# Turning h before the first mixer: a trip through DRAM and 32x32 turns on VectorE, in place of TensorE's transposes, with the norm vector in the split of w_in

## The reference, cut to what matters

```python
h = swiglu_half_step(h, ffn1_norm[i], ffn1_w_gate_up[i], ffn1_w_down[i])
z = rms_norm(h, mix_norm[i]) @ w_in[i]
z_mix, z_mem = z[..., :768], z[..., 768:]
y_mix = multiscale_pool_mixer(z_mix, pool_w[i], pool_scale[i])       # layer 0
y_mem = memory_attention(z_mem, mem, mem_norm[i], w_mem_kv[i], ...)
h = h + concatenate([y_mix, y_mem]) @ w_out[i]
```

## Time and profile before

| | us |
|---|---|
| median of 3 runs | 912.81 |
| lowest, highest run | 912.79, 912.90 |
| the profiled execution: its time | 912.87 |
| the profiled execution: its span | 910.8 |
| TensorE busy | 905.8 |
| VectorE busy | 635.5 |
| ScalarE busy | 501.3 |
| GpSimd busy | 107.2 |

### The profile page before, as it was taken

The page is one execution under the profiler, slowest core; times in us unless marked ns, Lnnn a source line. Parts: engine busy times, 40 slices in busy tenths (PEclk is TensorE's granted clock), DMA queues, the critical chain, the costliest instruction groups (busy, mean ns, idle before and its releaser), DMA issues.

```text
span 910.8 us, 15058 instructions
## 1 busy us (share of the span) xinstructions
PE 905.8 (99%) x4998; PEld 769.0 (84%) x4998; DVE 635.5 (70%) x970; ACT 501.3 (55%) x750; POOL 107.2 (12%) x186
## 2 busy tenths in 40 slices
PE   9999999999999999999999999999999999999998
PEld 6888888888888888888888888888888788888887
DVE  6766577687677766566778766656878776666665
ACT  6654455565655554454564645445676664545542
POOL 2052302003000000000002930000121000000000
PEclk9999999999999999999999999999999999999999
DMA  9897656556346656565375865665443276566551
GB/s 294 268 278 231 196 187 183 186 157 212 88 141 201 213 173 201 184 194 195 119 213 164 265 199 173 208 185 185 141 137 117 76 243 214 183 206 188 171 171 47
DMA packets 140195, 168.26 MB, mean 185 GB/s; under 512 B 12488, under 2 KB 104624, under 8 KB 140160
## 3 DMA queue, kind: packets, MB, share of 16 engines
q1 hardware_dynamic: 135616, 164.67, 56.9%
q0 software_dynamic: 4368, 3.07, 1.6%
q10 hardware_dynamic: 176, 0.07, 0.0%
HBM read 166.19 MB, written 1.05 MB: 184 GB/s over the span
## 4 chain that ended last, share of the span: by engine, by line
PE 99%; DVE 1%; ACT 0%; issue 0%; POOL 0%; ACTq 0%; POOLq 0%
PE ps L1763 35%; PE ps L1768 18%; PE ps L1977 8%; PE ps L1975 8%; PE ps L1973 8%; PE ps L1849 5%; PE ps L1851 5%; PE ps L1850 5%; PE ps L1733 1%; PE ps L2101 1%; PE ps L1802 1%; PE ps L2182 1%; PE ps L2070 0%; PE ps L1816 0%; PE ps L2139 0%; PE ps L2236 0%
## 5 line engine op out<-in xcount | busy, mean ns | idle before, releaser
L1763 PE MATMUL ps<-mainT,w_hi 128*128 128x512 f32 x1376 | 468.7, 393 | 0.2
L1148 DVE TENSOR_TENSOR w_lo<-w_raw,w_hi 128x1024 fp32r<-128x1024 f32 x296 | 350.7, 1221 | 42.6 <-ACT w_hi L739 42.2
L1768 PE MATMUL ps<-mainT,w_lo 128*128 128x256 f32 x1376 | 350.5, 280 | 0.0
L739 ACT CAST w_hi<-w_raw 128x1024 fp32r<-128x1024 f32 x296 | 299.7, 1047 | 28.3 <-PE ps L1763 11.2
L1763 PEld LDWEIGHTS ps<-mainT,w_hi 128*128 128x128 f32 x1376 | 248.9, 188 | 46.2 <-issue 0.5
L1768 PEld LDWEIGHTS ps<-mainT,w_lo 128*128 128x128 f32 x1376 | 255.8, 189 | 13.8
L797 ACT COPY gate_up_f<-ps 128x512 f32<-128x512 f32 x88 | 51.2, 582 | 105.0 <-PE ps L1763 99.6
L1240 DVE TENSOR_TENSOR gate_up_f<-ps,gate_up_f 128x256 f32<-128x256 f32 x88 | 37.2, 423 | 90.5 <-ACT gate_up_f L797 90.4
L1977 PE MATMUL ps<-w_hi,actT_lo 128*128 128x512 f32 x320 | 98.9, 390 | 0.0
L1975 PE MATMUL ps<-w_lo,actT_hi 128*128 128x512 f32 x320 | 98.9, 390 | 0.0
L1973 PE MATMUL ps<-w_hi,actT_hi 128*128 128x512 f32 x320 | 98.6, 389 | 0.0
(11 more groups left out here) (248 smaller groups left out, 844.0 us busy)
## 6 DMA issues: line engine op xcount, KB each, us to landing
w_raw<-in_ffn_w_gate_up_dram SPq DMA_DIRECT2D x352, 256.0 KB, 3.9
w_raw<-in_ffn_w_down_dram SPq DMA_DIRECT2D x176, 256.0 KB, 3.5
w_raw<-in_w_in_dram SPq DMA_DIRECT2D x32, 256.0 KB, 3.5
w_raw<-in_w_out_dram SPq DMA_DIRECT2D x32, 256.0 KB, 3.4
w_raw<-in_w_mem_kv_dram SPq DMA_DIRECT2D x16, 256.0 KB, 3.0
w_raw<-in_w_kv_dram SPq DMA_DIRECT2D x8, 256.0 KB, 3.5
ycat<-in_mem_dram SPq DMA_DIRECT2D x1, 1024.0 KB, 7.5
z<-in_mem_dram POOLq DMA_DIRECT2D x32, 32.0 KB, 4.1
```

What stands on the lines that cost most here:

```text
L739: ins = nc.scalar.copy(half(w_hi[s], b), half(w_raw[s], b))
L1148: ins = nc.vector.tensor_tensor(half(w_lo[s], b), half(w_raw[s], b), half(w_hi[s], b).bitcast(F32), ALU.subtract)
L1763: return pe.matmul(gate_sums(fb, j)[:, :, tokens], w_hi[units[k // 4][0]][:, k % 4, cols], both[:, k, :, tokens], start=start, stop=stop)
L1768: return pe.matmul(gate_sums(fb, j)[:, 0, tokens], w_lo[units[k // 4][0]][:, k % 4, cols], both[:, k, 0, tokens], start=False, stop=False)
```

## The change

For the norm H2 alone, TensorE's 16 transposes of h and VectorE's four multiplications by the norm vector go. In their place GpSimd, for one token tile after the other, waits for both halves of h, writes the tile (512 KB) to a tensor `h_rows` in DRAM, waits until this has landed, and issues four DMAs of 128 KB that read it back in blocks of 32 tokens by 32 columns into z, one DMA for each group of 32 partitions. The reads are made of 1024 runs of 128 bytes each. This stands ahead of `row_roots("H2")` on GpSimd. VectorE turns the blocks from z into ycat, two instructions of 128x512 a tile (`h_turns`), and ScalarE and VectorE split from there. The norm vector goes into the split of w_in's four units. On VectorE and ScalarE the work around it is put in another order, as the diff shows: on VectorE the turns and splits of tile 0 stand between the low parts of z0b's first and second unit, and the turns of tile 1 between the two halves of the second unit.

```diff
--- before.py
+++ after.py
@@ -113,14 +113,14 @@
 GAINS = 9
 FIRST_GAINS = 2
 
-WEIGHT_GAIN = {"mkv0": 2, "mkv1": 3}
-
-SPLIT_GAIN = {"H0": 0, "H45": 1, "H2": 4, "H7": 5, "H3": 6, "H8": 7, "K45": 8}
+WEIGHT_GAIN = {"mkv0": 2, "mkv1": 3, "z0a": 4, "z0b": 4}
+
+SPLIT_GAIN = {"H0": 0, "H45": 1, "H7": 5, "H3": 6, "H8": 7, "K45": 8}
 
 
 SUMS = ["H0", "M", "H2", "H3", "H45", "H7", "H8"]
-TURNS = ["H0", "H2", "H3", "H45", "H7", "Y1", "H8"]
-SCALES = ["H0", "H2", "H3", "K45", "H45", "H7", "H8"]
+TURNS = ["H0", "H3", "H45", "H7", "Y1", "H8"]
+SCALES = ["H0", "H3", "K45", "H45", "H7", "H8"]
 SPLITS = ["H0", "M", "H2", "H3", "K45", "H45", "H7", "Y1", "H8"]
 SPLIT_INTO = {"M": "side", "Y1": "y", "K45": "y"}
 
@@ -212,6 +212,9 @@
         h = sb("h", [P, NT, D])
         z = sb("z", [P, NT, D])
         ycat = sb("ycat", [P, NT, D])
+        h_blocks = [z[:, t, :].rearrange("p (k i c) -> p k i c", i=P // BLOCK, c=BLOCK) for t in range(NT)]
+        h_turned = [ycat[:, t, :].rearrange("p (k t) -> p k t", t=P) for t in range(NT)]
+        h_rows = nc.dram_tensor("h_rows", [S, D], F32, kind="Internal").ap()
         mem_blocks = z[:, :, :].rearrange("p t d -> p (t d)").rearrange("p (k t) -> p k t", t=S)
         key_blocks = ycat[:, 0, 0:NT * KVH * HD].rearrange("p (t c) -> p t c", t=NT)
         key_rows = ycat[:, 1, :].rearrange("p (n t) -> p n t", n=KVH)
@@ -284,6 +287,9 @@
         mem_blocks_landed = sem("mem_blocks_landed")
         mem_blocks_turned = sem("mem_blocks_turned")
         keys_landed = sem("keys_landed")
+        h_rows_landed = sem("h_rows_landed")
+        h_blocks_landed = sem("h_blocks_landed")
+        h_blocks_turned = [sem(f"h_blocks_turned{t}") for t in range(NT)]
         consts_landed = sem("consts_landed")
         ident_landed = sem("ident_landed")
         gains_landed = [sem(f"gains_landed{g}") for g in range(2)]
@@ -451,6 +457,8 @@
         def turned_view(name, t, b):
             if name == "M":
                 return mem_turned[b][:, :, t * P:(t + 1) * P]
+            if name == "H2":
+                return h_turned[t][:, 4 * b:4 * b + 4, :]
             return ps[:, turn_bank(name, t, b), :].rearrange("p (k t) -> p k t", k=4)
 
         def slots(r):
@@ -697,6 +705,16 @@
                             pool.dma_start(mem_blocks[q * BLOCK:(q + 1) * BLOCK, k, :].rearrange("f (i c) -> f i c", c=BLOCK),
                                            mem_tokens[:, :, cols]).then_inc(mem_blocks_landed, 16)
             row_roots("M")
+            for t in range(NT):
+                rows = slice(t * P, (t + 1) * P)
+                for b in range(2):
+                    pool.wait_ge(h_ready[t][b], STEP_OF["H2"])
+                pool.dma_start(h_rows[rows, :], h[:, t, :]).then_inc(h_rows_landed, 16)
+                pool.wait_ge(h_rows_landed, 16 * (t + 1))
+                tokens = h_rows[rows, :].rearrange("(i f) (k q c) -> q f k i c", f=BLOCK, q=BLOCKS, c=BLOCK)
+                for q in range(BLOCKS):
+                    pool.dma_start(h_blocks[t][q * BLOCK:(q + 1) * BLOCK, :, :, :],
+                                   tokens[q]).then_inc(h_blocks_landed, 16)
             row_roots("H2")
             head_roots("mk0")
             pool.wait_ge(consts_landed, 16 * SMALL_LOADS)
@@ -777,6 +795,9 @@
                 elif name == "M":
                     act.wait_ge(mem_blocks_turned, b + 1)
                     src = turned_view(name, t, b)
+                elif name == "H2":
+                    act.wait_ge(h_blocks_turned[t], b + 1)
+                    src = turned_view(name, t, b)
                 else:
                     act.wait_ge(turned[t][b], turn_no(name))
                     src = turned_view(name, t, b)
@@ -901,6 +922,11 @@
                                act_f[:, :, :].rearrange("p c n -> p (c n)")).then_inc(actT_hi_ready, 1)
                 if FOLLOWING[name] is not None:
                     high_unit(FOLLOWING[name], 1)
+                    if after == "H2":
+                        row_sum(after, 0)
+                        high_unit("z0b", 0)
+                        row_sum(after, 1)
+                        return
                     into = "K45" if after == "H45" else after
                     split(into, 0, 0)
                     row_sum(after, 0)
@@ -1045,8 +1071,11 @@
                 split(after, 1, 1)
 
             ffn(0, "H0", "H2")
-            high_unit("z0b", 0)
+            split("H2", 0, 0)
+            split("H2", 0, 1)
             high_unit("z0b", 1)
+            split("H2", 1, 0)
+            split("H2", 1, 1)
             high_unit("z0a", 0)
             z_copy(0, 1, 0)
             high_unit("z0a", 1)
@@ -1356,6 +1385,11 @@
                 low_unit(FOLLOWING[name], 1, (0,))
                 residual(r, norm, 0, 0)
                 residual(r, norm, 0, 1)
+                if after == "H2":
+                    low_unit(FOLLOWING[name], 1, (1,))
+                    residual(r, norm, 1, 0)
+                    residual(r, norm, 1, 1)
+                    return
                 scale(into, 0, 0)
                 split(into, 0, 0)
                 low_unit(FOLLOWING[name], 1, (1,))
@@ -1618,10 +1652,24 @@
                                                scalar=row_scale("H2", t), in1=zp_hi[:, t, cols].bitcast(F32),
                                                op0=ALU.mult, op1=ALU.subtract).then_inc(pool_lo_ready, 1)
 
+            def h_turns(t):
+
+                dve.wait_ge(h_blocks_landed, 16 * BLOCKS * (t + 1))
+                for b in range(2):
+                    nc.vector.transpose(ycat[:, t, b * 512:(b + 1) * 512], z[:, t, b * 512:(b + 1) * 512]).then_inc(
+                        h_blocks_turned[t], 1)
+
             low_unit("z0b", 0)
             mkv0 = (mkv_sb, mkv_done, mkv_ready, 0, "mkv0", "M", GU_BANK)
+            h_turns(0)
+            split("H2", 0, 0)
+            split("H2", 0, 1)
+            low_unit("z0b", 1, (0,))
             kv_copy(*mkv0, 0)
-            low_unit("z0b", 1)
+            h_turns(1)
+            low_unit("z0b", 1, (1,))
+            split("H2", 1, 0)
+            split("H2", 1, 1)
             kv_copy(*mkv0, 1)
             dve.wait_ge(mkv_ready, NT)
             head_sums("mk0")
@@ -2027,9 +2075,11 @@
                     end_bank(1, 0)
                     last_halves()
                     return
-                turn_h(after, 0, 0)
+                if after != "H2":
+                    turn_h(after, 0, 0)
                 end_bank(1, 0)
-                turn_h(after, 0, 1)
+                if after != "H2":
+                    turn_h(after, 0, 1)
                 end_bank(1, 1)
 
             def turn_heads(y):
@@ -2244,7 +2294,7 @@
             turn_first(1, 0)
             keep_warm(WARM_PRODUCTS[1])
             ffn(0, "H0", "H2")
-            projection("mkv0", "side", "M", GU_BANK, mkv_done, 0, late_tile("H2"))
+            projection("mkv0", "side", "M", GU_BANK, mkv_done, 0)
             projection("mkv0", "side", "M", GU_BANK + 1, mkv_done, 1)
             z0b = ("z0b", "main", "H2")
             projection(*z0b, z_bank(0, 0, 1), z_done, 0)
```

## The result

The changed kernel takes **920.3 us** in the median of 4 runs (919.6 to 920.52) against 912.8 (912.65 to 912.9) for the kernel before: ratio 1.008, interval 1.0068 to 1.0092, so 7.5 us slower (6.2 to 8.4). The forecast was 915.9, slower by 3.1, with 919.9 as its upper end: the sign is right, the size is not. The profiled execution took 920.52, its span is 918.6. One execution of e13 (4764 us) and one of e15 (1505 us) further down belong to another state of the chip and are left out of their figures.

What follows compares the result with a forecast made beforehand. TensorE, busy 99% of the span, was taken as the bound: 2.0 us saved on transposes against 5.0 us of waiting for the blocks gave +3.0 us on 912.87, so 915.9 us; range 911.9 to 919.9.

Steps and rivals of the forecast that it cites:

- The transposes: TensorE around the first mixer: removing the 16 transposes of h saves 2.0 us, and no more can be had.
- a wait at chunk 6: TensorE, 18 products into z0b: about 4.1 us of waiting for VectorE's low part behind tile 1's turns.
- L: Time when tile 1's fourth block read has landed: 209.2, where later than 204.25 makes TensorE lose time.
- the first write: GpSimd's 512 KB write of tile 0 to DRAM, beside weight loads: 4.5 us from 191.3.
- the second write: GpSimd's 512 KB write of tile 1 after 199, with the DMA taken as idle: 3.5 us.
- from there to the blocks: Tile 1 written at 203.3, its fourth read issued from 206.3, landing in 2.8 us with idle DMA: 209.2.
- Tile 0 is just in time: z0b's start: tile 0 turned and split at 203.8, where z0b would like to start at 203.9.
- Rival 4: The clock falls in TensorE's wait and slows products behind it, adding 1.4 to 3.4 us: 917.3 to 919.3; chance 0.12.
- the turns of the probabilities: TensorE's second, smaller gap, with VectorE late at the softmax maxima: the rest of 5.0 us after about 4.1.
- Rival 1: The DRAM trip is shorter, L 206 to 207.8, gain and wait about cancel: −0.3 to +1.5 us; chance 0.24.
- rival 2: The DRAM trip is hidden, L at most 204.4, and the 2.0 us are kept: 910.9 to 911.0; chance 0.09.
- Rival 3: Short runs are dear, reads and writes land late, L 215.0: +8.8 us, 921.6; chance 0.09.

Runs made afterwards that it cites:

- e13: e2 with 17 GpSimd memsets that hold z0b's start, so TensorE waits with nothing else late: 915.95 us, ratio 1.0032.
- e15: e10 with the memory projection's copies behind tile 1's splits and out0's low part behind the softmax maxima on VectorE: 912.72 us, ratio 0.9998.
- e2: Changed kernel without the writes to DRAM; blocks are read early from the input x in place of h: 910.7 us, ratio 0.9979.
- e5: Kernel before with only the norm vector moved into w_in's split; TensorE's transposes stay: 912.98 us, ratio 1.0003.
- e3: Changed kernel with both tiles' writes issued before any read, a semaphore for each tile: 917.55 us, ratio 1.0055.
- e10: Changed kernel with both writes first (e3), z0b's low part ahead of tile 1's turns (e4) and z0a's loads held (e9): 912.21 us, ratio 0.9995.
- e4: Changed kernel with the low part of z0b's second unit's second half ahead of tile 1's turns on VectorE: 918.06 us, ratio 1.0056.
- e9: Changed kernel with the SP queue's loads of z0a's weights held until tile 0's blocks are turned: 922.24 us, ratio 1.0102.
- e7: As e1, with 24 dummy products ahead of chunk 6 in place of 13: 919.78 us, ratio 1.0078.
- e14: e13 with 15 dummy products on TensorE ahead of the wait, same z0b start: 914.35 us, ratio 1.0017.
- e1: Changed kernel with dummy products of 512 columns on TensorE, 10 ahead of z0b and 13 ahead of its chunk 6: 920.23 us, ratio 1.0081.
- e8: Changed kernel with e4's order and four half-tile writes, each issued when ready, all ahead of the reads: 917.41 us, ratio 1.0052.
- e11: e2 with 13 GpSimd memsets that hold z0b's start: 911.87 us.
- e6: Changed kernel with only tile 1 through DRAM, tile 0 transposed on TensorE, and z0b's low parts before tile 1's turns: 911.51 us, ratio 0.9985.

## Why the prediction was wrong in size

**Right.** The transposes: 2.0 forecast, 2.1 measured (e2). The gain at nothing (e5). The structure: a wait at chunk 6 ended by the low part of w_in behind the turns of tile 1, and the loss following the time of the blocks (e3 and e10 move it as their blocks move, e4 moves what stands behind them). Issue of a read: 0.88 us apart, 1.0 taken from the line through the earlier trace rows. The DMA engines' own time for a tile's short runs: 2.3 us forecast, and GpSimd's queue holds 0.307 of the 7.31 us of tile 1's reads, 2.2 us.

**The step that failed: the landings in the sum for L.** By its terms, against the rows of after: start 191.84 for 191.3 (+0.5); the first write 5.84 for 4.5 (+1.3); its four issues 3.5 for 4.0 (−0.5); the second write 4.8 for 3.5 (+1.3); from there to the blocks 7.3 for 5.9 (+1.4). Together +4.05, which is L's 213.26 against 209.2. I took every term but the first write "with the DMA idle", because the earlier trace rows show 198 to 200 at 0.00. It was idle for none of them. The first write had been sized too short as well. What ran beside each:

- The first write, and the reads of tile 0 (6.7 us from first issue to the turns, for 5.8): w_in's loads. From 191.84 to 197.68 they hold 0.63 of the engines' time, from 197.68 to 204.40 0.36. The idle window was a property of the old order: the loads were paced by VectorE's low part, and the change moves that forward. I had listed "a weight load that moves earlier out of the way" as an argument *for* a shorter trip. It moved earlier into the way. Where the loads are held, the figures come out about as I had them: write 3.3 (e9), first four reads to turned 195.06 to 201.09 = 6.0 (e10).
- The second write: the trip's own reads of tile 0. From 201.18 to 205.95 weight loads hold 0.01 of the engines' time, GpSimd's queue 0.55. In e9, with the loads held, it still takes 202.81 − 198.51 = 4.3.
- The reads of tile 1: out0's loads, 0.21 of the engines' time against 0.31 for the reads. These are not newly in the way. Before, they were issued from 205.17 on and kept the engines busy:

```profile
206.00:208.00 2.00, 2.00 (x11) 1.65 (x10) 1.93 (x4) 1.05 (x1) 0.00 (x0) 1.00 0.91 265
```

The prediction held them up by some 5 us, to about 210, just behind its own L of 209.2. They are issued from 209.07 on, while the last read is still under way: it took 4.9 us to land where I had 2.8.

"Tile 0 is just in time" fell with the first of these: its turns start at 204.40 for 201.6.

**The second failed step: the sum had no clock in it.** Rival 4 had it, at 1.4 to 3.4 us and a chance of 0.12. The waits of 2.5 and 3.4 us both brought the clock to its lower level; only the second costs time, 1.6 us by the traces of e7 and by e13 against e14. The two causes are not alternatives but one: a wait long enough to be forecast is a wait in which the clock can fall, so it belonged in the forecast's own sum.

**A term that did not appear.** I put 0.9 us at the turns of the probabilities, VectorE being late there. After, VectorE's maxima wait 1.33 us for TensorE. One part is the slow products, which give VectorE time. The other is a sum that was too long: VectorE is ready for the maxima at 230.86, L + 17.6 and not L + 18.4, above all because GpSimd's roots come 2.9 us after the sums and not 3.9. In e7, at full clock, nothing is recorded as a wait there. In e4 and e10, where TensorE is less late, the wait is there, 0.48 and 0.49.

The account as it stands, of the profiled executions: chunk 6 at 215.91 where 208.0 was wanted, +7.9; clock behind it +1.6; transposes −2.0: **+7.5**, and measured is 7.5 (7.65 between the profiled executions). The forecast read 5.0 − 2.0. It is a reading of traces. That e1's and e7's medians lie only 0.1 and 0.5 below the changed kernel's, with the clock up in most or all of their executions, it does not explain.

Rival 1 (a shorter trip) and rival 2 (hidden) are out by L, 213.26, and the two waits. Rival 3 came nearest in us, 921.6. Its name is wrong: the short runs take 2.2 us of the engines a tile, and e10 makes the same reads with 0.31 us of wait. But it took its landings from crowded stretches, and those came: 4.2 us for the second write (4.8 measured) and 4.9 for the last read (4.9).

**Still open**: what the 1.5 us are that e10 stays behind e2; why e1's executions at full clock are no quicker than the changed kernel's, as only one execution of each was traced; and e15's median.

## What to carry to other kernels

An idle window of a resource belongs to the order that made it: before a transfer is put into it, ask which engine's step paces the others' transfers, and whether the change moves that step. Then ask what else is due to start before the transfer has landed, its own neighbours included. A trip through DRAM may take the place of TensorE's transposes for the tile that is wanted last, not for the one that is wanted next. And a forecast wait of TensorE like the ones here (2.5 to 4 us) needs a term for the clock behind it; it was 1.6 us here, and nothing where a second wait followed at once.

## What the runs showed of the hardware that was not expected

- In the profiled executions the clock fell behind waits of TensorE of 2.47, 2.65 (e4), 2.69 (e1), 3.21 (e13), 3.39, 3.47 (e3) and 4.05 us (e8), and not behind 0.88 (e11) and 1.73 (e4). The same wait does not always do it: by their mean clocks it fell in 8 of 10 executions of e13 and in 1 of 4 of e1. One fall cost 1.6 us of dense products of 512 columns (e13 against e14). Where products on unread data filled the wait, the clock stayed at 1.00 (e7, e14).
- A write of 512 KB from GpSimd's queue lands in 3.3 us with the weight loads held (e9) and in 5.8 among them. The Trainium skill ("DMA: Bandwidth & Descriptors", Anatomy of one DMA) gives an estimated 3.2 us for it; e9's 3.3 agrees, and the crowded 5.8 shows how far it reaches.
- Four reads of 128 KB in runs of 128 bytes take, from first issue to the turns, 6.0 (e10) and 6.3 us (e9) with no weight load beside them, 6.7 and 7.3 us in the changed kernel (loads at 0.36 and 0.21 of the engines' time), 7.8 in e6 (0.54), and 12.9 us where weight loads hold 0.71 of the engines' time (e9).
- A read made of 1024 runs of 128 bytes costs GpSimd some 0.9 us of issue, where a plain write of 512 KB costs 0.53 and 0.64 (e10). Four of them, 3.5 us, stand between the first write's landing and the second write.
